# Two transformer blocks on one core: expert 6's down weights in X, an earlier second down product, another order of the last expert loads, fillers in the last step

## The chip, the cores and the metric

One core of a Trainium2 chip. The metric is device time in microseconds of one execution; before the change three runs gave 914.12, 910.62 and 912.9, median 912.9. All times below that are read from a trace are counted from the start of the profiled span.

## The reference, cut to what matters

256 tokens of 1024 channels pass through two blocks. The first block is attention and a Hyena filter, a cross attention, and a mixture of experts; the second an RG-LRU and a block attention, and a mixture of experts. Both mixtures have 32 experts in 4 groups, each token takes two experts of its best group, and each expert is

```python
hdn = silu(x @ w_gate[e]) * (x @ w_up[e])      # 1024 -> 256, twice
y   = (hdn * weight_of_the_token) @ w_down[e]  # 256 -> 1024
```

All in float32. Gate and up weights of one expert are 2048 KB, down weights 1024 KB, so that one expert is 3 MB and the 32 of one mixture 96 MB. All experts are loaded, whatever the router chooses.

## The kernel before, in words

Each mixture runs one expert per step, 32 steps, experts in fixed order in the first mixture and in an order that may turn from step 8 in the second. Five queues (PE, ACT, DVE, POOL, SP) run hand-written programs that meet at semaphores. SP issues the weight transfers.

**Places for weights.** `ring` has four slots of 3 MB (`RING` = 4). The first mixture adds two more places (`apart`: 16 KB rows in `arena` for gate and up, `ROW` and `HT` for down), so it has six (`SIX` = 6), and expert e uses place e % 6. SP's `in_six` (L593) writes the refills: for expert e, wait until gate and up product e - 6 is done (semaphore `gu_done1`), issue gate and up weights, wait until down product e - 6 is done (`down_done1`), issue down weights. The first six experts are asked for ahead of that, the last of them behind the routing product `rt1`. The second mixture has the four slots and, for expert 4, a place made of `HT`, `X` and a part of `arena`. Its first loads are written out up to expert 11 (`first = 3 * RING`); ahead of the loop for experts 12 to 31 stands a `sp.wait_ge(sem("routed"), 3)` (L686).

**PE.** `first_steps` writes out steps 0 to 2, `step_of_six` is a step of the first mixture: turn the gate and up result of the step before (`turn`), turn the gathered rows of the step after (`gather_T`), gate and up product (`gated_up`, 16 matmuls of L1232), scatter the result of e - 2 to the tokens (`onto_tokens`, L1275), gather rows for e + 2 (`gather_rows`, L1198), down product of e - 1 (`brought_down`, L1247). `step` does the like in the second mixture (gate and up L1227, down L1247); it has the rows gathered ahead.

**DVE.** One iteration per step e: `hidden(e - 1)` (it needs gate and up of e - 1 turned by PE), `x_window(e + 1)`, `to_slots(e - 1)`, `low_part(e - 1)`. Four iterations carry a piece more: `extra_counts`, `extra_slots`, `extra_starts`, `extra_experts`, which work out the tiles of experts with more tokens than a window holds. In both mixtures these stand in iterations 4, 5, 6 and 7. In the first mixture they use `X` as scratch, in the second `XN`. `extra_experts` ends with an increment of `routed`. The semaphore gets three increments in the program: `extra_experts` of the first mixture (1), `order_of_steps` of the second in iteration 2 (2), `extra_experts` of the second (3).

```python
                sp.wait_ge(sem("routed"), 3)                        # SP, second mixture, L686
                with sp.Fori(first, NE - RING + 1, RING) as e0:
...
                    if e == RING:                                   # DVE, L2916, both mixtures
                        extra_counts()
...
                    elif e == RING + 3:
                        extra_experts()
```

**Behind the first mixture.** SP loads into freed slots, in this order: `ada10`, `win0`, `ada11`, `win2`, `win3`, ... (2048 KB each). PE runs `ada(10)`, transposes, `ada(11)` (both L903), then the projection with `win0` (L777 to L779). POOL issues the row `final_norm_g` into `ROW` behind a count of down products, and `gates_w` behind the first results of DVE; ACT issues two reads of `bias_rows`.

Of the kernel before, what the change touches and what calls it, by code (L numbers as in the profile page):

```python
# [46 lines left out]
NE = G * EPG  # L47
# [129 lines left out]
GU = 2 * KD * FE  # L177
FEAT = S + 2 * FFN


# [91 lines left out]
def two_blocks(nc, A, out):  # L272

    ctx = ExitStack()
    with ctx:
# [189 lines left out]
        def slot(i):  # L465
            return i % RING

        def arrived(eng, name):
            i = PLACE[name]
            eng.wait_ge(sem(f"slot_full{slot(i)}"), 16 * (i // RING + 1))  # L470
            return ring[:, slot(i), :]

        def vacated(sp, i):

            prev = i - RING
            if prev < 0:
                return
            for b, m in enumerate(MOE_AT):
                if m <= prev < m + RUNG[b]:
                    j = prev - m  # L480
                    sp.wait_ge(sem(f"down_done{b + 1}"), (SIX * (j // RING) + j % RING if b == 0 else j + (j >= RING)) + 1)
# [105 lines left out]
        def _(sp):  # L587
# [4 lines left out]
            def in_six(w):  # L592

                base = MOE_AT[0]

                def refill(e, q, src):
# [7 lines left out]
                    sp.wait_ge(sem("down_done1"), e - (SIX - 1))  # L604
                    if q < RING:
                        sp.dma_start(ring[:, s, GU:SLOT], src[:, GU:SLOT]).then_inc(sem(f"slot_down{q}"), 16)
                    else:
                        sp.dma_start(apart[q - RING][1], src[:, GU:SLOT]).then_inc(sem(f"beside_d{q - RING}"), 16)

                with sp.Fori(SIX, SIX * (NE // SIX) - SIX + 1, SIX) as e0:  # L610
                    for q in range(SIX):
                        refill(e0 + q, q, w[bass.ds(e0 + q, 1)].rearrange("a p f -> p (a f)"))
                for e in range(SIX * (NE // SIX), NE):
                    refill(e, e % SIX, w[e, :, :])

# [5 lines left out]
            def experts(b):  # L621
# [33 lines left out]
                if b == 0:  # L655
                    gate_beside(1, w[RING + 1, :, :])
                    filled("rt1")
                    down_beside(1, w[RING + 1, :, :])
                    in_six(w)
                    return extra_tiles(b, w, slot(base + 2), SIX * (NE // SIX) - RING)  # L660
                filled("rt2")
# [83 lines left out]
        def _(pe):  # L745
# [344 lines left out]
            def moe(b):  # L1090
# [199 lines left out]

                uses_1 = [-(-(NE - q) // SIX) for q in range(SIX)]

                def gate_of_six(n, r):
# [9 lines left out]
                def down_of_six(n, r):  # L1303

                    q, use = r % SIX, r // SIX
                    if q >= RING:
# [15 lines left out]
                def down_arrived(e, r):  # L1322

                    if isinstance(e, int) and e == RING:
                        pe.wait_ge(sem("beside_d0"), 16 * uses_1[RING] + 16)
# [3 lines left out]
                    pe.wait_ge(sem(f"slot_down{q}"), (e - r) * (16 // RING) + more + 16 * uses_1[q])  # L1329
                    return ring[:, slot(base + q), GU:SLOT]  # L1330
# [21 lines left out]
                def first_steps():  # L1352
# [18 lines left out]
                    turn(1)  # L1371
                    gated_up(0, 2)
                    gather_rows(3, 1)
                    onto_tokens(0, 0)
                    gather_T(3)
                    brought_down(0, 1)
                    gather_rows(4, 0)

                def step_of_six(n, r):
# [4 lines left out]
                    if not last:  # L1384
                        gather_T(e + 1)
                    gated_up(n, r)
                    onto_tokens(e - 2, r % 2)
# [788 lines left out]
        def _(dve):  # L2176
# [409 lines left out]
            def moe(b):  # L2586
# [312 lines left out]
                if b == 1:  # L2899
# [7 lines left out]
                    times_up(hb).then_inc(sem("hb1"), 1)  # L2907
                for e in range(3 - b, 2 * RING):
                    if b == 1 and e == 2:
# [4 lines left out]
                    if b == 2 and e == 2:  # L2914
                        order_of_steps()
                    if e == RING:  # L2916
                        extra_counts()
                    elif e == RING + 1:
                        extra_slots()
                    elif e == RING + 2:  # L2920
                        extra_starts()
                    elif e == RING + 3:
                        extra_experts()
# [18 lines left out]

                experts(2 * RING, NE - RING)
                last_step = NE - 1
# [351 lines left out]
        def _(pool):  # L3296
# [58 lines left out]
            pool.wait_ge(sem("mask_row"), 1)  # L3355
            pool.wait_ge(sem("down_done1"), SIX * (NE // SIX) - 1)
            broadcast_row(ROW[:, 0:1024], "final_norm_g", D, "rows")
# [101 lines left out]
```

## Time and profile before

| | us |
|---|---|
| median of three runs | 912.9 |
| profiled execution, its own time | 910.73 |
| its span | 908.9 |
| PE busy in the span | 860.0 (95%) |
| DVE busy | 532.9 (59%) |
| ACT busy | 362.2 (40%) |
| DMA, mean over the span | 314 GB/s |

The span lies 1.8 us under the time of its own execution. PE counts as busy while matmuls are in its pipeline, so its share says little about slack; the DMA row by slices and the waits tell more. The span falls into the first block up to about 300 us, its mixture to about 518, the second block's mixers to about 670, and the second mixture to about 898.

### The profile page before, as it was taken

To read this page: it belongs to the slowest core of one execution; us is meant where nothing else is said; L and a number is where in the kernel's file an instruction comes from. 1 tells how busy PE (TensorE), PEld (TensorE's weight loads), DVE (VectorE), ACT (ScalarE), POOL (GpSimd) and SP (SyncE) were. 2 spreads that over 40 slices of the span, in tenths; PEclk is the share of its full clock that TensorE was granted. 3 is DMA by queue.
4 is the path that set the end of the run, shared out by engine and by line. 5 is a ranking of instruction groups with operands and counts; after the bars stand their busy time and mean duration, and the time that the engine had idled before them with its cause. 6 is when DMAs were issued, how large, how long until landed. Compare 5 with 4: busy or idle time off the path is not lost.

```text
span 908.9 us, 15580 instructions
## 1 busy us (share of the span) xinstructions
PE 860.0 (95%) x5774; PEld 541.0 (60%) x5774; DVE 532.9 (59%) x1182; ACT 362.2 (40%) x711; POOL 22.3 (2%) x41
## 2 busy tenths in 40 slices
PE   8999999999999898999978799999899999999995
PEld 7778558887977333444433389876664555455552
DVE  5877669465455757555554476888754643333335
ACT  5674435455354232333322457745521111111113
POOL 1010111000000000000000000000000000000000
PEclk9999999999999999999999899999999999999998
DMA  9655895546656799999999986630769899999991
GB/s 350 261 192 221 319 393 203 187 176 244 258 204 269 310 368 422 424 426 426 426 424 423 423 317 270 231 140 1 314 228 375 332 412 423 425 425 424 427 416 51
DMA packets 28903, 285.38 MB, mean 314 GB/s; under 512 B 3080, under 2 KB 5544, under 8 KB 7856
## 3 DMA queue, kind: packets, MB, share of 16 engines
q1 hardware_dynamic: 25344, 278.25, 75.6%
q0 software_dynamic: 1136, 3.74, 1.2%
q10 hardware_dynamic: 2368, 2.64, 0.9%
q8 instruction: 36, 0.59, 0.3%
q14 instruction: 19, 0.16, 0.0%
HBM read 283.56 MB, written 1.06 MB: 313 GB/s over the span
## 4 chain that ended last, share of the span: by engine, by line
PE 71%; DVE 12%; DMA 9%; ACT 4%; issue 2%; SPq 0%; DVEq 0%; ACTq 0%
PE bank L1227 13%; PE bank L1247 8%; DMA ring<-in_experts 8%; PE bank L777 8%; PE bank L779 7%; PE bank L778 7%; PE bank L1275 6%; PE bank L1232 4%; DVE ring_r L529 2%; PE bank L1239 2%; PE bank L1198 2%; PE bank L903 1%; PE bank L754 1%; DMA ring<-in_lat 1%; PE bank L868 1%
## 5 line engine op out<-in xcount | busy, mean ns | idle before, releaser
L529 DVE TENSOR_TENSOR ring_r<-ring,ring_r 128x1024 fp32r<-128x1024 f32 (+1 forms) x84 | 99.4, 1212 | 65.4 <-ACT ring_r L522 65.2
L1227 PE MATMUL bank<-ring,arena 128*64 128x256 f32 x992 | 113.9, 382 | 0.6 <-DVE arena L2724 0.6
L522 ACT ACTIVATE ring_r<-ring 128x1024 fp32r<-128x1024 f32 (+1 forms) x84 | 84.9, 1046 | 67.6 <-PE bank L779 66.6
L777 PE MATMUL bank<-HT_r,ring_r 128*128 128x256 f32 x352 | 102.0, 290 | 1.9 <-DVE ring_r L529 1.1
L779 PE MATMUL bank<-HT_r,ring_r 128*128 128x256 f32 x352 | 99.6, 283 | 0.0
L1227 PEld LDWEIGHTS bank<-ring,arena 128*64 128x64 f32 x992 | 68.9, 137 | 36.9 <-issue 5.9
L1247 PE MATMUL bank<-ring,arena 128*64 128x512 f32 (+1 forms) x424 | 83.7, 609 | 1.0 <-issue 0.6
L778 PE MATMUL bank<-XN_r,ring_r 128*128 128x256 f32 x288 | 81.5, 283 | 0.0
L1275 PE MATMUL bank<-arena_r 64*128 64x512 f32 x496 | 75.1, 421 | 2.9 <-DVE arena_r L2808 2.4
L1934 ACT ACTIVATE arena<-bank 128x512 f32<-128x512 f32 (+1 forms) x64 | 31.5, 491 | 113.1 <-PE bank L1227 79.9
L2801 DVE SCALAR_TENSOR_TENSOR arena<-bank,arena 128x512 f32<-128x512 f32 x32 | 24.0, 750 | 83.3 <-PE bank L1247 83.3
L1275 PEld LDWEIGHTS bank<-arena_r 64*128 64x128 f32 x496 | 42.2, 186 | 48.0 <-issue 35.0
L777 PEld LDWEIGHTS bank<-HT_r,ring_r 128*128 128x128 f32 x352 | 67.4, 192 | 5.3 <-issue 5.2
L779 PEld LDWEIGHTS bank<-HT_r,ring_r 128*128 128x128 f32 x352 | 67.5, 192 | 0.0
L1949 ACT ACTIVATE arena_r<-arena 128x512 fp32r<-128x512 f32 x31 | 19.5, 629 | 103.4 <-DVE arena L2801 103.4
L1232 PE MATMUL bank<-ring,arena 128*32 128x512 f32 x352 | 44.0, 619 | 12.5 <-DMA ring<-in_experts 10.2
L2808 DVE SCALAR_TENSOR_TENSOR arena_r<-bank,arena,arena_r 128x512 fp32r<-128x512 f32 x31 | 23.2, 750 | 55.6 <-ACT arena_r L1948 55.6
L778 PEld LDWEIGHTS bank<-XN_r,ring_r 128*128 128x128 f32 x288 | 55.2, 192 | 1.0 <-issue 1.0
L1239 PEld LDWEIGHTS bank<-tab,arena 128*128 128x128 f32 x192 | 19.9, 141 | 52.1 <-issue 51.4
L1247 PEld LDWEIGHTS bank<-ring,arena 128*64 128x64 f32 (+1 forms) x424 | 20.8, 126 | 42.6 <-issue 41.2
L777 PE MATMUL bank<-ring_r,HT_r 128*128 128x512 f32 (+1 forms) x96 | 37.5, 391 | 1.8 <-DVE ring_r L529 1.4
L779 PE MATMUL bank<-ring_r,arena_r 128*128 128x512 f32 x96 | 37.6, 391 | 0.0
(507 smaller groups left out, 1442.0 us busy)
## 6 DMA issues: line engine op xcount, KB each, us to landing
ring<-in_experts SPq DMA_DIRECT2D x53, 2048.0 KB, 13.3
ring<-in_experts SPq DMA_DIRECT2D x53, 1024.0 KB, 10.3
ring<-in_ada SPq DMA_DIRECT2D x12, 2048.0 KB, 10.0
arena<-in_experts SPq DMA_DIRECT2D x10, 2048.0 KB, 16.9
ring<-in_win SPq DMA_DIRECT2D x5, 2048.0 KB, 12.6
ring<-in_hy SPq DMA_DIRECT2D x3, 2048.0 KB, 17.9
HT<-in_experts SPq DMA_DIRECT2D x6, 1024.0 KB, 13.5
ROW<-in_experts SPq DMA_DIRECT2D x5, 1024.0 KB, 13.4
```

Source lines behind the costliest of these rows:

```text
L522: nc.scalar.activation(R(h), w, ACT.Copy).then_inc(sem("w_high"), 1)
L529: nc.vector.tensor_tensor(R(w), w, R(h), ALU.subtract).then_inc(sem("w_low"), 1)
L777: mm(ps, R(ah), R(bh), start=first, stop=False)
L778: mm(ps, R(ah), R(bl), start=False, stop=False)
L779: return mm(ps, R(al), R(bh), start=False, stop=last_)
L1227: last = mm(gu_bank[g * wide:(g + 1) * wide, 0:256], xw[:, k, :], w[k // 4][:, k % 4, g * 256:(g + 1) * 256], start=k == 0, stop=k == KD - 1)
L1232: last = mm(gu_bank[g:g + wide, :], xw[:, 2 * (k % 4) + k // 4, :], w[k // 4][:, k % 4, :], start=k < sides, stop=k >= KD - sides)
L1239: last = tr(guT_bank[:, c * P:(c + 1) * P], gu_sb[:, c * P:(c + 1) * P], ident)
L1247: last = mm(d_bank[g:g + wide, :], hb[:, f, :], w[:, o:o + 512], start=b == 1 or f == 0, stop=b == 1 or f == 1)
L1275: last = mm(acc[2 * t + h][:, :], R(onto[b][rows, i, t * P:(t + 1) * P]), R(u[rows, :]), start=False, stop=False)
L1934: A_(gu_sb[:, 0:gu_cols], gu_bank[:, 0:gu_cols], ACT.Copy).then_inc(sem(f"gu_sb{b}"), 1)
L2801: return V.scalar_tensor_tensor(out=y_gated, in0=(d_bank if bank is None else bank)[:, :], scalar=cur[:, i, 1:2], in1=g2half, op0=ALU.mult ...
```

## The change

- `freed_1` and new place numbers: gate and up of expert e stay at place e % 6. Down weights of expert 6 go to `X`; down weights of the experts behind it go to place (e - 1) % 6, so each waits, in the first round, for one down product fewer.
- SP issues expert 6's down weights to `X` behind the counting product `cns1`, ahead of the refills.
- In the last refills the order is gate and up 30, gate and up 31, down 30, down 31.
- The loads of `ada10`, `win0` and `ada11`, and POOL's `final_norm_g`, wait for one down product more.
- PE: `brought_down(0, 1)` stands straight behind `gated_up(0, 2)`, with a wait for `y_low1`.
- PE: five matmuls of 128x256 (fillers) stand ahead of the gate and up product of the last step.
- DVE: the written-out iterations go to `looped` = (5 - b) * RING, 16 in the first mixture and 12 in the second, and the four extra pieces stand in the last four of them: 12 to 15 in the first, 8 to 11 in the second.

```diff
+        def freed_1(j):
+            q = j % RING
+            e = SIX * (j // RING) + q
+            return max(e, max(d for d in range(SIX + 1, NE) if (d - 1) % SIX == q) if e + SIX >= NE else e + 1)
...
-                with sp.Fori(SIX, SIX * (NE // SIX) - SIX + 1, SIX) as e0:
...
+                refill_gate(SIX, 0, w[SIX, :, :])
+                for e in range(SIX + 1, 2 * SIX + 1):
+                    refill_gate(e, e % SIX, w[e, :, :])
+                    refill_down(e, (e - 1) % SIX, w[e, :, :], SIX + 1)
+                with sp.Fori(2 * SIX + 1, NE - 2 * SIX, SIX) as e0:
...
+                for e in range(NE - SIX - 1, NE - 1):
+                    refill_gate(e, e % SIX, w[e, :, :])
+                    if e == NE - 2:
+                        refill_gate(NE - 1, (NE - 1) % SIX, w[NE - 1, :, :])
+                    refill_down(e, (e - 1) % SIX, w[e, :, :])
+                refill_down(NE - 1, (NE - 2) % SIX, w[NE - 1, :, :])
...
+                    filled("cns1")
+                    sp.dma_start(X[:, :, :].rearrange("p t d -> p (t d)"), w[SIX, :, GU:SLOT]).then_inc(sem("down_in_x"), 16)
                     in_six(w)
...
                     gated_up(0, 2)
+                    pe.wait_ge(sem("y_low1"), 1)
+                    brought_down(0, 1)
                     gather_rows(3, 1)
                     onto_tokens(0, 0)
                     gather_T(3)
-                    brought_down(0, 1)
...
+                    if last:
+                        for _ in range(FILL):
+                            mm(gu_bank[:, 0:256], ident, T("iota")[:, 0:256], start=True, stop=True)
                     gated_up(n, r)
...
-                for e in range(3 - b, 2 * RING):
+                looped = (5 - b) * RING
+                for e in range(3 - b, looped):
...
-                    if e == RING:
+                    if e == looped - 4:
                         extra_counts()
...
-                    elif e == RING + 3:
+                    elif e == looped - 1:
                         extra_experts()
...
-                experts(2 * RING, NE - RING)
+                experts(looped, NE - RING)
...
-            pool.wait_ge(sem("down_done1"), SIX * (NE // SIX) - 1)
+            pool.wait_ge(sem("down_done1"), SIX * (NE // SIX))
```

## Rows read from the trace of the kernel before

**Rows 1.** The page, transfer rate of the core in 40 equal slices.
```profile
GB/s 350 261 192 221 319 393 203 187 176 244 258 204 269 310 368 422 424 426 426 426 424 423 423 317 270 231 140 1 314 228 375 332 412 423 425 425 424 427 416 51
```

**Rows 2.** SP's queue in time: start us, us, issuing line, out<-in.
```profile
307.59 0.34 SPq L601 DMA_DIRECT2D ring<-in_experts  x1
...
313.41 0.33 SPq L601 DMA_DIRECT2D ring<-in_experts  x1
322.80 0.33 SPq L606 DMA_DIRECT2D ring<-in_experts  x1
...
514.25 0.33 SPq L590 DMA_DIRECT2D ring<-in_ada  x1
```

**Rows 3.** Stretches of the first mixture: engines, then PE clock, DMA share, GB/s.
```profile
305.00:310.00 5.00, 4.06 (x32) 1.64 (x32) 3.74 (x19) 2.49 (x5) 0.00 (x0) 1.00 0.31 66
...
320.00:325.00 5.00, 4.50 (x35) 2.04 (x36) 2.60 (x7) 1.74 (x3) 0.00 (x0) 1.00 0.61 205
...
333.00:505.00 172.00, 157.46 (x1272) 63.53 (x1268) 97.68 (x240) 56.97 (x107) 0.58 (x1) 0.99 1.01 424
```

**Rows 4.** PE in time, first mixture and behind; in brackets idle before, releaser.
```profile
317.12 1.92 PE L1232 MATMUL bank<-ring,arena 128*32 128x512 f32 x16 [0.99 <-DVE arena L2601]
...
430.20 1.93 PE L1232 MATMUL bank<-ring,arena 128*32 128x512 f32 x16
...
453.64 1.92 PE L1232 MATMUL bank<-ring,arena 128*32 128x512 f32 x16
...
498.28 1.92 PE L1232 MATMUL bank<-ring,arena 128*32 128x512 f32 x16 [1.48 <-DMA ring<-in_experts]
...
506.96 3.64 PE L1232 MATMUL bank<-ring,arena 128*32 128x512 f32 x16 [4.04 <-DMA ring<-in_experts]
...
514.52 1.06 PE L1247 MATMUL bank<-ring,arena 128*32 128x512 f32 x8 [0.33 <-DVE arena L2746]
...
526.17 1.92 PE L903 MATMUL bank<-ring,cm 128*32 128x512 f32 x16
```

**Rows 5.** PE in time, the matmuls that have the fillers' shape.
```profile
518.15 1.99 PE L754 MATMUL bank<-tab 128*128 128x256 f32 x8
```

**Rows 6.** POOL's and ACT's issues in time, behind the first mixture.
```profile
496.37 0.58 POOL L3323 DMA_DIRECT2D ROW<-in_final_norm_g  x1 [229.78 <-PE bank L1247]
521.49 0.55 POOL L3359 DMA_DIRECT2D ROW<-in_gates_w  x1 [24.54 <-DVE X L3021]
...
523.44 0.41 ACTq L2034 DMA_DIRECT2D arena<-bias_rows  x1
```

**Rows 7.** Transfers issued from 480 to 560 us: count, KB each, median us to landing.
```profile
arena<-bias_rows ACTq DMA_DIRECT2D x1, 1024.0 KB, 14.1
...
ROW<-in_gates_w POOLq DMA_DIRECT2D x1, 512.0 KB, 11.8
```

**Rows 8.** SP's queue in the second mixture, last written-out load and first looped one.
```profile
732.10 0.33 SPq L685 DMA_DIRECT2D ring<-in_experts  x1
733.45 0.33 SPq L693 DMA_DIRECT2D ring<-in_experts  x1
```

**Rows 9.** DVE in time: hidden of step 6, end of extra_experts, hidden of step 10.
```profile
720.09 0.28 DVE L2747 TENSOR_TENSOR arena<-arena,bank 128x128 f32<-128x128 f32 x1
...
721.85 0.13 DVE L2896 CAST tabi<-arena 1x1 int32<-1x1 f32 x1
...
747.96 0.28 DVE L2747 TENSOR_TENSOR arena<-arena,bank 128x128 f32<-128x128 f32 x1
```

**Rows 10.** The chain of waits, gate and up products of experts 12 and 31.
```profile
753.20 3.60 PE bank L1227 x32
...
886.40 3.60 PE bank L1227 x32
```

**Rows 11.** Stretches of the second mixture, columns as in rows 3.
```profile
720.00:885.00 165.00, 165.00 (x1186) 84.21 (x1180) 62.84 (x154) 27.54 (x70) 0.00 (x0) 1.00 1.01 423
...
885.00:886.00 1.00, 1.00 (x10) 0.88 (x9) 0.75 (x1) 0.00 (x0) 0.00 (x0) 1.00 0.75 311
```

More of the change, by code:

```diff
@@ L178 @@
 FEAT = S + 2 * FFN
+FILL = 5
 STAGES = [("f1", 1, (1,)), ("hT", 4, (6, 7, 2, 4)), ("lat", 2, (3, 0)), ("f2", 1, (5,)), ("f3_0", 4, (1, 6, 7, 2)),
@@ L480, in vacated @@
                     j = prev - m
-                    sp.wait_ge(sem(f"down_done{b + 1}"), (SIX * (j // RING) + j % RING if b == 0 else j + (j >= RING)) + 1)
+                    sp.wait_ge(sem(f"down_done{b + 1}"), (freed_1(j) if b == 0 else j + (j >= RING)) + 1)
                     return
@@ L594, in in_six, with refill_gate @@
                 base = MOE_AT[0]
-                def refill(e, q, src):
+                def refill_gate(e, q, src):
                     s = slot(base + q)
@@ L603, in refill, with refill_down @@
                         sp.dma_start(apart[q - RING][0], src[:, 0:GU]).then_inc(sem(f"beside_gu{q - RING}"), 16)
-                    sp.wait_ge(sem("down_done1"), e - (SIX - 1))
+                def refill_down(e, q, src, places=SIX):
+                    sp.wait_ge(sem("down_done1"), e - (places - 1))
                     if q < RING:
-                        sp.dma_start(ring[:, s, GU:SLOT], src[:, GU:SLOT]).then_inc(sem(f"slot_down{q}"), 16)
+                        sp.dma_start(ring[:, slot(base + q), GU:SLOT], src[:, GU:SLOT]).then_inc(sem(f"slot_down{q}"), 16)
                     else:
                         sp.dma_start(apart[q - RING][1], src[:, GU:SLOT]).then_inc(sem(f"beside_d{q - RING}"), 16)
-                with sp.Fori(SIX, SIX * (NE // SIX) - SIX + 1, SIX) as e0:
-                    for q in range(SIX):
-                        refill(e0 + q, q, w[bass.ds(e0 + q, 1)].rearrange("a p f -> p (a f)"))
-                for e in range(SIX * (NE // SIX), NE):
-                    refill(e, e % SIX, w[e, :, :])
+                refill_gate(SIX, 0, w[SIX, :, :])
[3 more added lines that the diff above has]
+                with sp.Fori(2 * SIX + 1, NE - 2 * SIX, SIX) as e0:
+                    for q in range(SIX):
+                        src = w[bass.ds(e0 + q, 1)].rearrange("a p f -> p (a f)")
+                        refill_gate(e0 + q, (q + 1) % SIX, src)
+                        refill_down(e0 + q, q, src)
+                for e in range(NE - SIX - 1, NE - 1):
[4 more added lines that the diff above has]
+                refill_down(NE - 1, (NE - 2) % SIX, w[NE - 1, :, :])
             def half_outside(w, q):
@@ L658, in experts @@
                     down_beside(1, w[RING + 1, :, :])
+                    filled("cns1")
+                    sp.dma_start(X[:, :, :].rearrange("p t d -> p (t d)"), w[SIX, :, GU:SLOT]).then_inc(sem("down_in_x"), 16)
                     in_six(w)
-                    return extra_tiles(b, w, slot(base + 2), SIX * (NE // SIX) - RING)
+                    return extra_tiles(b, w, slot(base + 2), SIX * (NE // SIX) - RING + 1)
                 filled("rt2")
@@ L1291, in moe @@
                 uses_1 = [-(-(NE - q) // SIX) for q in range(SIX)]
+                downs_1 = [-(-(NE - 1 - q) // SIX) for q in range(SIX)]
                 def gate_of_six(n, r):
@@ L1303, in down_of_six @@
                 def down_of_six(n, r):
+                    if r == SIX and isinstance(n, int):
+                        pe.wait_ge(sem("down_in_x"), 16)
+                        return X[:, :, :].rearrange("p t d -> p (t d)")
+                    if r > SIX or not isinstance(n, int):
+                        r = r - 1
                     q, use = r % SIX, r // SIX
@@ L1324, in down_arrived @@
                     if isinstance(e, int) and e == RING:
-                        pe.wait_ge(sem("beside_d0"), 16 * uses_1[RING] + 16)
+                        pe.wait_ge(sem("beside_d0"), 16 * downs_1[RING] + 16)
                         return outside[1]
@@ L1328, in down_arrived @@
                     more = 0 if r < ways and in_turn(e) else 16
-                    pe.wait_ge(sem(f"slot_down{q}"), (e - r) * (16 // RING) + more + 16 * uses_1[q])
+                    pe.wait_ge(sem(f"slot_down{q}"), (e - r) * (16 // RING) + more + 16 * downs_1[q])
                     return ring[:, slot(base + q), GU:SLOT]
@@ L2915, in moe @@
                         order_of_steps()
-                    if e == RING:
+                    if e == looped - 4:
                         extra_counts()
-                    elif e == RING + 1:
+                    elif e == looped - 3:
                         extra_slots()
-                    elif e == RING + 2:
+                    elif e == looped - 2:
                         extra_starts()
-                    elif e == RING + 3:
+                    elif e == looped - 1:
                         extra_experts()
```

## The prediction, made before the changed kernel was run

> **What bounds the kernel now.** I read four views in this order. The page's rate by slices first: the core moves about 424 GB/s from slice 16 to 23, falls to 1 in slice 28, and is at 423 or more again from slice 33 on [rows 1]. These two plateaus are the mixtures; the stages between use less than the bandwidth. Then PE in time, to see which plateau PE waits in. In the first mixture a step costs PE (453.64 - 430.20) / 4 = 5.86 us when it waits for nothing [rows 4], while 3 MB at 424 GB/s take 7.42 us; PE runs ahead on what was loaded early, and in the end waits, 1.48 us at step 30 (498.28) and 4.04 us at step 31 (506.96) [rows 4]. That stage ends on the last weights. In the second mixture gate and up of expert 12 start at 753.20 and of expert 31 at 886.40 [rows 10]: 133.2 us over 19 steps, less 0.84 us for a list product in the last one, is 6.97 us a step, with PE busy all 165 us of the stretch [rows 11]. It is bound by PE, but barely: DMA carries 423 GB/s throughout [rows 11], and 3 MB an expert then take 7.45 us. PE lives on a lead that shrinks by 0.48 us a step. Third, the SP queue, for what starts each transfer. Last, single rows where the change puts a new wait.
>
> **First mixture, the stream of weights.** SP asks for expert 6's gate and up at 307.59, and until then DMA has nothing: 305 to 310 moved 66 GB/s, so (1 - 66/424) x 5 = 4.2 us are lost. A second hole is 320 to 325, 205 GB/s, 2.6 us [rows 3]: the down weights of expert 7 are asked for only at 322.80 and gate and up of 8, queued behind them on SP, later still, though the third gate and up product was over at 319.04 (317.12 + 1.92) [rows 2, 4]. From an issue to full flow I take 1.64 us, an estimate: 205 GB/s in 320 to 325 leave 2.6 us of hole, which fits an end near 321.8 and a new start at 324.44, 1.64 behind 322.80 [rows 2, 3].
>
> Now the changed order. Down 6 (1 MB, 2.47 us) is asked for near 302 and fills part of the first hole. Gate and up 6 flow from 307.59 + 1.64 = 309.23 to 314.17; those of 7, issued 313.41, from 315.05 to 319.99; down 7 no longer waits for the second down product and follows to 322.46. Gate and up 8 can be asked for at about 319.3 and follow without a hole. Before, down 7 flowed from 324.44 to 326.91, so gate and up 8 start 4.45 us earlier. Later places come free in time: gate and up 9 need the fourth gate and up product (near 328.2), and would flow from 329.9, which is when down 8 ends. The cost of the moved down product: the rows for step 3 are gathered 1 us later, which puts step 3 about 0.95 us later. PE's lead over the stream hides it; uncovered it would be 0.95 us. The extra DVE pieces stop PE for some us wherever they stand. In step 12 PE would be at 326.2 + 9 x 5.86 = 378.9, its weights land at 322.46 + 4.94 + 4 x 7.42 = 357.1: a lead of over 20 us hides them, so I count nothing. Stream: 4.4 us earlier; bounds 2.5 (only down 6 counts) and 5.4.
>
> **First mixture, its end.** Gate and up 30 land 4.4 us earlier, and PE starts them at 493.9 instead of 498.28 [rows 4]. Between them and those of 31 stood 1 MB of down 30 (2.47 us) and the row `final_norm_g`, issued 496.37 [rows 6] (0.5 MB, 1.24 us). Both now come behind: gate and up 31 land at 493.85 + 4.94 = 498.8. PE is through step 30 and the turn at about 493.9 + 4.6 = 498.5 (a step's 5.86 less the gathering that the last steps no longer have). Five fillers follow; eight of that shape take 1.99 us, of which the last stays 0.35 us in the pipeline, so 0.23 us each and 1.2 us in all [rows 5]: 0.9 us of them beyond the landing. The product of step 31 starts at 499.7 and takes 1.92 us as at 498.28, not 3.64 as at 506.96, where the wait of 4.04 us had left the granted clock near its 1.2 GHz level [rows 4]. The last down product starts at the later of its hidden values (499.7 + 1.92 + 3.0 = 504.6; before, 3.92 us from 510.60 to 514.52, of which I put 0.9 to the slow clock) and its weights (498.8 + 4.94 + 1.24 = 505.0): 505.0 against 514.52 [rows 4], 9.5 us earlier. Fillers dropped would not change that, as the weights decide.
>
> What is late next: the stream. `ada11` is the third 2 MB behind the experts. Before, issued 514.25 [rows 2], it landed by the order of the stream at 506.9 + 2.47 + 3 x 4.94 = 524.2, and PE used it without a wait at 526.17 [rows 4]. So 2.0 us of slack. With the stream 4.4 us earlier `ada11` lands at 519.8, PE would want it at 526.17 - 9.5 = 516.7 and waits. Besides, `gates_w` (before at 521.49) and the reads of `bias_rows` (523.44), 2 MB together, are issued by engines that run 9.5 us earlier [rows 6], so that they now lie beside `win0` and `ada11`. They took 11.8 and 14.1 us to land [rows 7]; over the 6 to 8 us that overlap I give them about half, 2.3 us of stream time. `ada11` then lands at 522.1, a gain of 4.1 us for all that follows; bounds 1.4 (all 2 MB ahead of it, 4.9 us) and 6.4 (none). The later waits of `ada10` and `win0` are hidden, as both have a queue of over 10 us ahead of them. From here PE has no waits for DMA and the gain is carried to the second mixture.
>
> On that sharing the Trainium skill (DMA: Bandwidth & Descriptors, Queues, rings and completion order) says that each DMA engine goes round-robin between its queue rows, packet by packet. The landing times in rows 7 agree that another queue's transfer neither waits for SP's queue nor overtakes it. By the rule alone, with the small packets of `bias_rows`, those reads would take less than my half, and the gain would be nearer 4.7.
>
> **Second mixture: the step that costs.** SP waits for `routed` = 3 before it asks for the weights of expert 12. Before, `extra_experts` stood in DVE's iteration 7, ended at 721.98 (721.85 + 0.13) [rows 9], and SP came to the wait at 732.4, behind down 11 (732.10), found it fulfilled, and issued at 733.45 [rows 8]. Now it stands in iteration 11, behind `hidden(10)`, whose product was at 747.96; from there to the end of `extra_experts` are 721.98 - 720.09 = 1.89 us [rows 9]. So `routed` = 3 comes at 749.85. SP needs about 1.0 us from the wait to the issue (733.45 - 732.43) [rows 8]: issue at 750.95, flow from 752.6. Before, with the queue never empty, the last 20 experts (60 MB, 62.9 million bytes) ended at 886.3 (the last row shows 0.75 us of activity and the microsecond behind it a third) [rows 11]; at 421 GB/s they take 149.5 us, so gate and up 12 flowed from 736.8. The stream falls back 752.6 - 736.8 = 15.8 us. What absorbs part of it is the lead at the end: gate and up 31 landed 2.47 us before the end, at 883.8, PE wanted them at 886.40 [rows 10], 2.6 us. Price 15.8 - 2.6 = 13.2 us. From the front: expert 12 lands at 757.5 instead of before 753.20, 4.3 us of wait, and then 19 steps of 0.48 us are 9.1, together 13.4. The two agree; I take 13.0, for some tenths in SP's path. All SP loads from 12 on are queued behind the waiting instruction; PE's step 12, and ACT and DVE by it, wait for them. Bounds: 10.5 (the flow resumes 2.5 us sooner) and 16 (the PE lead gone, and a slow clock behind the wait of 4.3 us). That slow clock: after 4.04 us of wait the product took 1.72 us more (3.64 against 1.92) [rows 4]; the same here puts PE behind the stream by a few us, which 0.48 us a step regain by step 31.
>
> Here a rule of the Trainium skill speaks against the change (TensorE: Matmul & The Clock Gate, HAM oscillation): a matmul loop that waits for DMA in every pass can fall to the low clock in every pass. Rows 4 show a product at full speed behind a wait of 1.48 us, so with 0.48 us a step I expect no such thing; were it so, the steps would double to 13.9 us.
>
> **Sum.** Against the profiled execution's own 910.73 us (span 908.9 plus 1.8): -4.1 + 13.0 = +8.9, 919.6. The median of the runs shown is 912.9, 2.2 above that execution; the same difference on it gives 921.8, which I predict.
>
> **Rivals.**
> *The late mark costs nothing (the other side).* Place: L686. The delay is free if expert 12's stream resumes before 736.8 + 2.6 = 739.4, that is if the mark comes by 736.7. Against it: hidden of step 10 cannot exist before 747.96 [rows 9], and nothing in the change touches the wait. For it only that I read the code and have no row of the late mark. Then the first mixture's gain stands alone: 912.9 - 4.1 = 908.8, or 903.4 if its full 9.5 came through. Decides above 739.4. Chance 0.08.
> *The first mixture's full gain comes through.* `ada11` isn't late, the reads don't get in its way: -9.5 + 13.0 = +3.5, 916.4. Against it: 524.2 against 516.7. Chance 0.10.
> *No gain in the first mixture.* `gates_w` and `bias_rows` push `ada11` back, or PE is late in the middle by the extra pieces: +13.0, 925.9. Chance 0.12.
> *Every step of the second mixture at the low clock:* 20 steps x 6 us, about 1,035. Rows 4 speak against it. Chance 0.01.
> Forecast as worked out: 0.69.
>
> **Range.** Terms at their bounds give +4.1 (10.5 - 6.4) to +14.6 (16 - 1.4). From 912.9 that is 917.0 to 927.5; the low end goes down to 914 to take in most of the full-gain case. 914 to 927.5.
>
> **Chances.** A difference under 0.5% (4.6 us) can't be told from none here. Faster by more: most of the case in which the mark costs nothing, 0.06. Within: the rest of it, the full-gain case and a small tail of the forecast, 0.14. Slower: 0.80.
>
> **What would show it.** Right: SP's first L693 issue about 17 us behind L685's sixth instead of 1.35, a hole of about 15 us in the DMA rate near 735 to 750 (4 us earlier by the gain), one PE wait of 3 to 5 us at gate and up 12, then waits of about half a microsecond each step. In the first mixture: no hole at 320, gate and up 31 at full clock, last down product near 505, a PE wait of 3 to 6 us for `ada11`. Wrong: no wait on `routed` in SP's rows, or the second L903 group at 526 as before.

## The result and the profile after

The changed kernel takes 922.08 us (median of four runs, 919.74 to 923.77), the kernel before on the same chip 912.51 (910.62 to 914.12): ratio 1.0104 with a 95% interval of 1.0074 to 1.0134, or 9.5 us slower by the ratio (9.6 by the medians). Forecast were 921.8 and +8.9. The profiled execution of the changed kernel is the slowest of its four: 923.77 us, span 921.9.

About 3 us of its span have nothing to do with the change. Windows of the changed kernel, its start; columns here and below: stretch in us, length, busy us of PE, PEld, DVE, ACT and POOL with instructions, granted PE clock, DMA share, GB/s.

```profile
10.00:20.00 10.00, 10.00 (x41) 8.64 (x40) 7.32 (x16) 6.29 (x12) 0.00 (x0) 0.67 0.99 419
```

Before, the same stretch had a granted clock of 1.00, and the first `ada` load was issued at 25.02; here it is issued at 28.38 (in the twelve other profiles at 25.1 to 25.9). So I count moments from that load in each execution, and give the difference to before:

| | after | after with one number changed (e1_again) |
|---|---|---|
| gate and up 30 start | -3.6 | -5.0 |
| last down product of the first mixture | -8.2 | -9.5 |
| `ada(11)` product | -5.2 | -5.4 |
| first gate and up of the second mixture | -5.0 | -6.2 |
| end of the span | +9.6 | -6.3 |

The first mixture and the stage behind it give about 5 us, the second mixture takes 14.7. The page's rate by slices has the loss in slice 33 of 40, 172 GB/s where it was 412 [rows 1] (the low slices 27 and 28 belong to the second block's mixers and were there before):

```profile
GB/s 352 242 172 205 332 388 213 183 182 240 263 194 284 348 410 421 423 425 424 429 423 422 423 307 210 225 49 91 320 279 405 321 172 429 424 427 423 424 422 57
```

Slice 33 is 738 to 761 us. By windows, after; the first two are the stretches of [rows 3], 305 to 310 and 320 to 325, moved by the 3.36 us of the later start:

```profile
308.36:313.36 5.00, 4.07 (x32) 1.63 (x32) 3.73 (x19) 2.44 (x5) 0.00 (x0) 1.00 0.68 224
323.36:328.36 5.00, 4.13 (x36) 1.74 (x27) 1.74 (x5) 1.13 (x2) 0.00 (x0) 1.00 1.03 439
735.00:740.00 5.00, 5.00 (x38) 2.38 (x36) 2.83 (x8) 0.79 (x2) 0.00 (x0) 1.00 0.31 126
740.00:745.00 5.00, 5.00 (x36) 2.25 (x34) 3.57 (x12) 0.39 (x1) 0.00 (x0) 1.00 0.01 2
745.00:750.00 5.00, 5.00 (x42) 2.84 (x40) 2.46 (x10) 1.18 (x3) 0.00 (x0) 1.00 0.01 2
755.00:760.00 5.00, 2.98 (x14) 1.72 (x16) 0.52 (x2) 0.00 (x0) 0.00 (x0) 0.50 1.03 436
```

The first hole of [rows 3] is filled about half, 224 GB/s for 66, and the second wholly, 439 for 205. A new one of 14.8 us stands between 736.5 (126 GB/s over 735 to 740) and 751.3 (1.64 behind the issue below). Why it is there is shown by DVE's and SP's rows (time, duration, engine, line, operation, tiles). Line numbers have moved: L685 is L707, L693 is L715, L1227 is L1249, L1232 is L1254, L1247 is L1269, L903 is L925.

```profile
746.35 0.28 DVE L2779 TENSOR_TENSOR arena<-arena,bank 128x128 f32<-128x128 f32 x1
748.11 0.14 DVE L2928 CAST tabi<-arena 1x1 int32<-1x1 f32 x1
...
730.43 0.33 SPq L707 DMA_DIRECT2D ring<-in_experts  x1
749.62 0.34 SPq L715 DMA_DIRECT2D ring<-in_experts  x1
```

The mark `routed` = 3 comes with the end of the cast, 748.25, 1.9 us behind the start of the `hidden` of step 10. SP, which was through with its last written-out load at 730.76, issues the first of the loop at 749.62. The waits of SP between 700 and 800 have the line (who waits, for whom: us in total, times, longest; L709 is the loop behind the wait):

```profile
SPq L709 <- DVE tabi L2928: 17.5, 1, 17.5
```

PE pays for it once at expert 12, and from expert 17 (794.10) to expert 30 in every step ("[... <-DMA" is the wait ahead of the group):

```profile
757.01 5.44 PE L1249 MATMUL bank<-ring,arena 128*64 128x256 f32 x32 [5.50 <-DMA ring<-in_experts]
765.76 3.67 PE L1249 MATMUL bank<-ring,arena 128*64 128x256 f32 x32
...
786.67 3.67 PE L1249 MATMUL bank<-ring,arena 128*64 128x256 f32 x32
794.10 3.67 PE L1249 MATMUL bank<-ring,arena 128*64 128x256 f32 x32 [0.39 <-DMA ring<-in_experts]
...
875.46 3.67 PE L1249 MATMUL bank<-ring,arena 128*64 128x256 f32 x32 [0.36 <-DMA ring<-in_experts]
884.10 3.67 PE L1249 MATMUL bank<-ring,arena 128*64 128x256 f32 x32 [1.61 <-DMA ring<-in_experts]
891.51 3.67 PE L1249 MATMUL bank<-ring,arena 128*64 128x256 f32 x32 [0.37 <-DMA ring<-in_experts]
899.34 3.67 PE L1249 MATMUL bank<-ring,arena 128*64 128x256 f32 x32
```

From 765.76 to 786.67 PE still goes at its own 6.97 us a step. From 794.10 to 875.46 are 11 steps of 7.40 us: 3 MB at 425 GB/s. The stage was bound by PE at 6.97 us a step [rows 10, 11]; from expert 17 on it is bound by DMA.

The end of the first mixture answers to [rows 4]:

```profile
498.02 1.92 PE L1254 MATMUL bank<-ring,arena 128*32 128x512 f32 x16 [1.47 <-DMA ring<-in_experts]
502.49 2.32 PE L1417 MATMUL bank<-tab 128*128 128x256 f32 x10
504.74 1.92 PE L1254 MATMUL bank<-ring,arena 128*32 128x512 f32 x16
509.71 1.06 PE L1269 MATMUL bank<-ring,arena 128*32 128x512 f32 x8 [0.34 <-DVE arena L2778]
517.70 3.12 PE L925 MATMUL bank<-ring,cm 128*32 128x512 f32 x16 [2.36 <-DVE st L3063]
524.34 1.92 PE L925 MATMUL bank<-ring,cm 128*32 128x512 f32 x16 [1.19 <-DMA ring<-in_ada]
```

With 3.36 us taken off for the later start, the last down product is at 506.35 instead of 514.52 and `ada(11)` at 520.98 instead of 526.17: of 8.2 us there are 5.2 left.

### The profile page after: what moved, and what is told of

Its sections match the earlier page's. It is cut to its first block, busy times and chain, and to the rows that moved or that the text cites. A ratio compares the mean times of both kernels' runs of the same rounds, so it can differ in the third digit from the quotient of the medians.

```text
span 921.9 us, 15486 instructions
## 1 busy us (share of the span) xinstructions
PE 865.0 (94%) x5784; PEld 550.3 (60%) x5784; DVE 532.3 (58%) x1182; ACT 362.0 (39%) x711; POOL 22.2 (2%) x41
## 4 chain that ended last, share of the span: by engine, by line
PE 63%; DMA 16%; DVE 12%; ACT 4%; issue 3%; SPq 1%; DVEq 1%; ACTq 0%
DMA ring<-in_experts 14%; PE bank L799 8%; PE bank L1249 7%; PE bank L801 7%; PE bank L800 7%; PE bank L1269 6%; PE bank L1254 4%; PE bank L1297 4%; PE bank L1220 2%; DVE ring_r L536 2%; PE bank L1261 2%; DMA ring<-in_ada 1%; PE bank L925 1%; PE bank L1226 1%; PE bank L890 1%
## 5 line engine op out<-in xcount | busy, mean ns | idle before, releaser
L1249 PE MATMUL bank<-ring,arena 128*64 128x256 f32 x992 | 115.7, 386 | 12.4 <-DMA ring<-in_experts 11.8
L1249 PEld LDWEIGHTS bank<-ring,arena 128*64 128x64 f32 x992 | 74.9, 138 | 45.5 <-issue 12.9
L1269 PE MATMUL bank<-ring,arena 128*64 128x512 f32 (+1 forms) x416 | 81.7, 600 | 1.0 <-issue 0.6
L1254 PE MATMUL bank<-ring,arena 128*32 128x512 f32 x352 | 42.3, 598 | 4.6 <-DMA ring<-in_experts 2.3
L1269 PEld LDWEIGHTS bank<-ring,arena 128*64 128x64 f32 (+1 forms) x416 | 20.4, 125 | 42.6 <-issue 40.3
```

Of the source, the lines that this page charges most:

```text
L1249: last = mm(gu_bank[g * wide:(g + 1) * wide, 0:256], xw[:, k, :], w[k // 4][:, k % 4, g * 256:(g + 1) * 256], start=k == 0, stop=k == KD - 1)
L1254: last = mm(gu_bank[g:g + wide, :], xw[:, 2 * (k % 4) + k // 4, :], w[k // 4][:, k % 4, :], start=k < sides, stop=k >= KD - sides)
L1269: last = mm(d_bank[g:g + wide, :], hb[:, f, :], w[:, o:o + 512], start=b == 1 or f == 0, stop=b == 1 or f == 1)
```

## The experiments

Each time is a median beside the kernel before on the same chip, with the ratio and its 95% interval. "Base" is e1: the changed kernel with the one number of e1. The disputed price first.

**e1, e1_again: the loop does not wait for the late mark.** The entries of the table that SP reads are written before the second increment.

```diff
-                sp.wait_ge(sem("routed"), 3)
+                sp.wait_ge(sem("routed"), 2)
```

> The changed kernel with one number changed: SP waits for routed = 2 ahead of its loop over experts 12 to 31, not for 3. DVE's extra pieces stay in iterations 8 to 11. Theory (SP's late mark is the whole price of the second mixture, 14.6 us in the trace): 922.1 - 14.6 = 907.5 us, no hole in DMA near 740, gate and up 12 start 27.9 us behind those of expert 8 (4 steps of 6.97), no wait there. Rival (the pieces themselves, now in iterations 8 to 11, hold up DVE and through it PE): the time stays above 915 with waits of PE on DVE in steps 8 to 12. Rival (the late start of the stream has another cause on SP): the hole stays.

Measured: 905.87 (904.91 to 909.09) against 911.43, ratio 0.9939 (0.9925 to 0.9953); on another chip, with twelve runs,

> The changed kernel with the wait for routed = 2 once more, as the base on the same chip as the two kernels with it: 0.994 of the kernel before, 905 to 907 us.

906.92 against 910.85, 0.9959 (0.9944 to 0.9973). In e1's windows the hole is gone:

```profile
740.00:745.00 5.00, 5.00 (x34) 2.27 (x32) 3.05 (x10) 0.90 (x2) 0.00 (x0) 1.00 1.01 424
```

One number turns +1.0% into -0.4 to -0.6%. So the wait of SP is what makes the changed kernel slower; the difference of the ratios, 0.0145 to 0.0165, is 13 to 15 us.

**e2: the pieces of the second mixture back in iterations 4 to 7, the wait kept.**

```diff
-                looped = (5 - b) * RING
+                looped = (6 - 2 * b) * RING
```

> The changed kernel with the extra pieces of the second mixture back in iterations 4 to 7 (looped = 16 in the first mixture, 8 in the second), the wait for routed = 3 kept. Theory: the mark comes near 720 and SP finds it there; 907.5 us, the same as with the wait for 2 within 1 us. If the pieces cost something of their own in 8 to 11, this one is faster than the wait for 2 by that much. Against the kernel before it shows the first mixture's changes alone: 4 to 6 us faster.

Measured: 907.67, 0.9960 (0.9944 to 0.9975). The mark early removes the loss as not waiting for it does. The medians of e1 and e2 on this chip are 1.8 us apart, more than the 1 us expected, but the intervals overlap and e1_again has nearly the ratio of e2; pieces that cost something of their own in iterations 8 to 11 would have made e2 the faster one.

**e3: the kernel before with nothing but the late pieces in the second mixture.**

```diff
+                looped = (1 + b) * RING
-                    if e == RING:
+                    if e == looped - 4:
                         extra_counts()
```

> The kernel before with only this change: the pieces of the second mixture in iterations 8 to 11 (the first mixture keeps 4 to 7). Theory: the late mark alone, 912.5 + 14.6 = 927.1 us, SP's first looped load about 17 us later, a PE wait of 4 to 6 us at gate and up 12. Rival (the two parts interact, the price exists only with the first mixture's changes): under 920.

Measured: 924.21 (923.5 to 926.9), 1.0148 (1.0127 to 1.0168). The first mixture is that of before, and the price appears all the same: 12.8 us by the medians, 13.5 by the ratio, and 14.1 in the trace from the first gate and up of the second mixture to the end, for the 14.6 expected. Up to there this kernel does what the one before does, and yet its profile is 0.9 us ahead: so much do two profiles differ by themselves. Its SP and PE:

```profile
SPq L687 <- DVE tabi L2896: 17.4, 1, 17.4
...
757.99 5.21 PE L1227 MATMUL bank<-ring,arena 128*64 128x256 f32 x32 [5.15 <-DMA ring<-in_experts]
```

**e10: how the price grows.** The changed kernel with the pieces of the second mixture one iteration earlier, in 7 to 10.

```diff
-                    if e == looped - 4:
+                    if e == looped - 4 - (b - 1):
```

> The changed kernel with the extra pieces of the second mixture one iteration earlier, 7 to 10 instead of 8 to 11; the wait for routed = 3 stays. The mark comes one step, 6.97 us, earlier. Theory (price = how late the stream resumes less the lead PE has at the end): 6.97 us less, 922.1 - 7.0 = 915.1 us, SP's first looped load 6.97 us earlier, the wait at gate and up 12 gone (5.5 - 7.0 below zero) and PE waits only from about step 15 on. Rival (the price is the one long wait and the slow clock behind it, about 7 us): nearly all of 14.6 us gone, about 908.

Measured: 914.04 against 911.37, 1.0029 (1.0018 to 1.0041). Its SP and its first wait:

```profile
727.54 0.33 SPq L707 DMA_DIRECT2D ring<-in_experts  x1
739.69 0.34 SPq L715 DMA_DIRECT2D ring<-in_experts  x1
...
776.83 3.67 PE L1249 MATMUL bank<-ring,arena 128*64 128x256 f32 x32 [0.25 <-DMA ring<-in_experts]
```

PE has no wait at step 12 here, and is overtaken at step 16. Counted from the first gate and up of the second mixture in each execution, SP's first load of the loop comes at 61.15 us before, 71.95 in e10, 79.0 in the changed kernel, and the stage from there to the end of the span takes 236.6, 244.1 and 251.3. A lateness of 10.8 us costs 7.5, one of 17.85 costs 14.7: 3.3 and 3.2 us are free, the rest is paid one for one. Without the late mark the same stretch takes 236.5 to 237.6 us in the ten profiles of the other runs on base, so that each of these figures is good to about a microsecond.

**e4: no fillers.** Base, `FILL = 5` to `FILL = 0`.

> The changed kernel with SP's wait for routed = 2 (905.9 us, called the base here) and no fillers ahead of the last gate and up product. Theory (weights decide the end of the mixture, and ada11 behind it): the product of step 31 starts about 1.2 to 2.2 us sooner, the wait ahead of it is under a microsecond so that it keeps the full clock, the last down product by its weights or hidden values at most 2 us sooner, and nothing of it arrives behind ada11: within 0.7 us of the base. Rival (the fillers keep the clock): a 3.6 us product, 1.5 us or more slower.

Measured: 906.36 against 911.14, 0.9942 (0.9924 to 0.9959).

```profile
500.02 1.92 PE L1254 MATMUL bank<-ring,arena 128*32 128x512 f32 x16 [1.24 <-DMA ring<-in_experts]
505.98 1.06 PE L1269 MATMUL bank<-ring,arena 128*32 128x512 f32 x8 [1.33 <-DMA ring<-in_experts]
```

Without them PE waits 1.24 us and the product of step 31 still takes 1.92 us. It starts 5.87 us behind the product of step 30 (494.15), with the fillers 6.72 us behind it (493.74 to 500.46 in e1_again): they take PE's wait and run 0.85 us beyond it. That is hidden, as without them the last down product waits 1.33 us for its weights, and starts 11.83 us behind the product of step 30, with them 11.68. They neither cost nor give anything that can be measured.

**e5: gate and up 31 behind down 30 again.** Base, with the two requests in the old order.

```diff
-                    if e == NE - 2:
-                        refill_gate(NE - 1, (NE - 1) % SIX, w[NE - 1, :, :])
                     refill_down(e, (e - 1) % SIX, w[e, :, :])
+                refill_gate(NE - 1, (NE - 1) % SIX, w[NE - 1, :, :])
                 refill_down(NE - 1, (NE - 2) % SIX, w[NE - 1, :, :])
```

> The base with the last loads in the old order: gate and up 30, down 30, gate and up 31, down 31. Theory: gate and up 31 land 2.5 us later, the last down product 2 to 4 us later, but ada11 lands when it did, as the bytes ahead of it are the same: total within 1 us of the base. Rival (the end of the mixture carries through): 2.5 us or more slower.

Measured: 906.73, 0.9952 (0.9933 to 0.9970). In its profile the first refill was 1.7 us later than in e4 beside it, and gate and up 30 by 1.8. The last down product comes 6.1 us earlier than before, 9.0 in e4; 1.8 of the difference go with the refill, which leaves 1.1 for the order, less than the 2 to 4 us expected and hardly more than two profiles differ by. At the second mixture's first gate and up e5 has 4.6 us, e4 3.9, in spite of the refill. So the order moves the last down product by a microsecond or less, and nothing of it is seen behind `ada11`.

**e6: the second down product back in its old place.** Base, `brought_down(0, 1)` behind `gather_T(3)`.

> The base with the second down product back behind the scatter. Theory: down 8 waits about 2.5 us longer on SP but the queue holds gate and up 8 then, so the hole does not come back (down 7 no longer waits for that product): stream and total within 0.7 us of the base, step 3 about 1 us earlier. Rival (it is this move that closes the hole at 320): 2.5 us slower.

Measured: 904.96 (904.72 to 906.02), 0.9925 (0.9902 to 0.9948), the lowest time of all. With both changes of place for weights in, the moved product brings nothing: gate and up 9 are asked for 19.8 us behind gate and up 6 in e6 (327.55 - 307.76) and 20.9 in e1_again (328.75 - 307.90, and the like in the other profiles with the moved product), since PE's work of step 3 comes about a microsecond later with it. The intervals of e6 and of base overlap, so that it is faster than base isn't shown; that the edit is not needed is.

**e7: expert 6's down weights not ahead of gate and up 6, but behind.** Base otherwise.

```diff
+                sp.dma_start(X[:, :, :].rearrange("p t d -> p (t d)"), w[SIX, :, GU:SLOT]).then_inc(sem("down_in_x"), 16)
```

> The base with expert 6's down weights asked for behind its gate and up weights, not ahead: the first hole of DMA isn't used. Theory (the stream's start decides when ada11 lands): 2.47 us lost less the 0.9 us gap behind gate and up 6, so gate and up 30 and ada11 1.6 to 2.5 us later, total 1.6 to 2.5 us above the base. Rival (the gain comes from the end of the mixture): no difference.

Measured: 908.62, 0.9958 (0.9942 to 0.9975): by the ratio not to be told from base, by the medians 1.7 us above e1_again. The 1.6 to 2.5 us expected are neither shown nor excluded. Windows of e7:

```profile
305.00:310.00 5.00, 3.63 (x31) 1.41 (x31) 3.77 (x18) 2.68 (x4) 0.00 (x0) 1.00 0.25 54
330.00:335.00 5.00, 5.00 (x44) 1.81 (x44) 1.77 (x5) 1.54 (x3) 0.00 (x0) 1.00 1.05 436
```

and of base (e1_again):

```profile
305.00:310.00 5.00, 4.00 (x32) 1.63 (x32) 3.83 (x18) 2.68 (x4) 0.00 (x0) 1.00 0.69 223
330.00:335.00 5.00, 5.00 (x44) 2.02 (x38) 2.16 (x4) 1.93 (x4) 0.00 (x0) 1.00 0.96 360
```

Base moves (223 - 54) x 5 = 845 KB more in the first stretch, worth 2.0 us, and loses part of it in the other, (436 - 360) x 5 = 380 KB or 0.9 us, where the queue waits for the gate and up product held back by the moved down product. At gate and up 30 the two differ by 1.1 us.

**Where the 9 us at the end of the first mixture shrink to 5.** e8 keeps PE busy with 12 fillers ahead of `ada(11)`, for its clock; e11 does so with 6; e9 puts `ada(11)` behind the projection with `win0`. All on base.

> The changed kernel with the wait for routed = 2, and 12 matmuls of 128x256 ahead of ada(11), where PE waits for that load. They take 2.8 us, less than the wait of about 4 us. Theory (the wait for ada11 costs twice: the wait, and a product and some matmuls at the low clock behind it): L925 at 1.92 us instead of up to 3.64, 1.5 to 2.3 us faster than the base where its wait was long, on average 1 to 2. Rival: no difference.

> The changed kernel with the wait for routed = 2 and 6 instead of 12 matmuls of 128x256 ahead of ada(11). A trace showed that each takes two records of 0.23 us, so 12 took 5.35 us and ran past the landing by 2.5 us; 6 take 2.7 us and end before it. Theory: L925 at 1.92 us in every execution, up to 2 us faster than the same kernel without them (906.5), 905.5 in the median. Rival (the execution time hangs on other clock events as much): within 0.7 us of 906.5.

> The changed kernel with the wait for routed = 2, and ada(11) and its column product moved behind the projection with win0 (ACT's copy of its result moved likewise). If ada11's landing is what holds back the gain of the first mixture, PE starts the projection as soon as win0 is split, near 521, and the total falls by 2 to 4 us below the base, to about 903. If something else holds it (win0, the split on ACT and DVE, final_norm_g), less than 1 us.

Measured: e8 908.89, 0.9970 (0.9956 to 0.9984); e11 905.88, 0.9942 (0.9927 to 0.9957); e9 906.47, 0.9946 (0.9929 to 0.9963). In e8 I had the fillers wrong in size:

```profile
518.44 5.35 PE L776 MATMUL bank<-tab 128*128 128x256 f32 x24
```

A matmul of this float32 shape is two records of 0.22 us, so 12 took 5.35 us where I had reckoned 2.8 from [rows 5]; they reached past the landing of the weights, and e8 tests nothing but that. In e11 the six fit:

```profile
519.60 2.76 PE L776 MATMUL bank<-tab 128*128 128x256 f32 x12
522.28 1.92 PE L925 MATMUL bank<-ring,cm 128*32 128x512 f32 x16
```

What they guard against is seen in e2 and, without it, in e1_again:

```profile
521.64 3.64 PE L925 MATMUL bank<-ring,cm 128*32 128x512 f32 x16 [4.05 <-DMA ring<-in_ada]
```
```profile
513.08 3.58 PE L925 MATMUL bank<-ring,cm 128*32 128x512 f32 x16 [2.04 <-DVE st L3063]
521.23 1.92 PE L925 MATMUL bank<-ring,cm 128*32 128x512 f32 x16 [2.67 <-DMA ring<-in_ada]
```

Over the profiles of the changed kernel and its variants, `ada(11)` took 3.64, 3.41, 3.44 and 2.75 us behind waits of 4.05 (e2), 3.71 (e4), 3.19 (e7) and 2.83 (e1), and 1.92 behind waits of 2.67, 2.49 (e6), 2.33 (e10), 2.24 (e5) and 1.19 (after). The wait is mostly shorter where `ada(10)` before it ran at the low clock, as in e1_again's first row (1.19, 2.49 and 2.67 us behind a slow one, 2.33 to 4.05 behind one of 1.92): that seems to cost nothing, as PE would wait for `ada11` anyway. Where `ada(11)` is the slow one, a gain of 4.6 us there has shrunk to 3.2 at the second mixture's first load in e2, while in e1_again 5.4 grew to 6.2; e4 (slow, 4.6 to 3.9) and e11 (fast, 4.8 to 5.6) go the same two ways. Base does now the one, now the other, which may be part of its scatter (904.51 to 910.95); that it is was not shown, for e11's interval overlaps base's two, and its median lies within 0.7 us of the 906.5 that its expectation compares with. In e9 PE goes from the transposes straight to the projection and waits for DVE there:

```profile
521.13 0.36 PE L799 MATMUL bank<-HT_r,ring_r 128*128 128x256 f32 x1 [1.91 <-DVE XN_r L3099]
```

The wait for `ada11` is replaced by one for DVE's split of the values, and `ada(11)` now costs its 1.92 us in a stretch where PE has work. The 2 to 4 us that e9 would have given if `ada11` alone held the stage did not come. e9 and e11 differ by 0.6 us in median, with overlapping intervals.

## Why the prediction was right

The forecast of 921.8 met 922.08, and its two terms were each close. That they met to 0.3 us is luck: in the traces the first part gave 5.0 us for 4.1 and the second cost 14.7 for 13.0, two errors of opposite sign, and the four runs lie 4 us apart. Point by point:

*The stream of the first mixture, 4.4 us earlier: right within the scatter.* In seven executions with all the edits that bear on the stream and no late first refill (after, e1_again, e2, e4, e8, e9, e11), gate and up 30 start 3.6, 5.0, 4.9, 4.6, 4.8, 4.3 and 4.5 us earlier. The first hole is filled in part and the second wholly, as reckoned. That the moved down product costs nothing was wrong: e6 has 5.8 us without it. I had it hidden by PE's lead, but SP's queue waits for the same gate and up products. My own reckoning had the place, the request for gate and up 9 just as the queue runs dry (329.9); that left no room for 1 us of delay, and the dip at 330 to 335 in base is what it cost.

*The last down product, 9.5 us earlier: right* (8.2 in the changed kernel, 8.8 to 9.5 in e1_again, e2, e4, e8, e9 and e11). What comes last there was a close call, as in the sum (504.6 against 505.0): the hidden values in the changed kernel (0.34 us behind DVE), the weights without fillers (e4).

*Fillers, 1.2 us: wrong, 2.32.* [Rows 5] count x8 records, and I took a record for a matmul. They run 0.85 us past PE's wait, for the 0.9 reckoned, but only because that wait is 1.24 us without them and not 0.3; the last down product does not see it, so that the error cost nothing. e4 shows also that they were not needed: a product behind a wait of 1.24 us takes 1.92 us, like that behind 1.48 us in [rows 4].

*`ada11` gives 4.1 of the 9.5 us on: right as a place, low in size.* `ada(11)` comes 5.2 us earlier in the changed kernel and 4.6 to 5.4 in e1_again, e2, e4 and e11. The whole gain by the ratios of e1, e1_again, e2 and e4 is 5.6, 3.7, 3.6 and 5.3 us, around and above the 4.1. The Trainium skill (DMA: Bandwidth & Descriptors, Queues, rings and completion order) says that each DMA engine takes its queue rows in turn, packet by packet. From that I had worked out that the reads of `bias_rows` take less of the stream than half their size, and a gain of 4.7; the traces, 4.6 to 5.4, lie on both sides of that, and don't decide it. I did not see two things. `final_norm_g` is now asked for at 502.67, and DVE waits for it ahead of the first values of the next stage, 1.37 us in e2, hidden, it seems, behind `ada11`. It is 1.82 us in the changed kernel. And the wait for `ada11` can leave PE at the low clock, which costs what e2 lost, about 1.5 us. The rival in which the full 9.5 us come through fell, as did the one without any gain.

*The second mixture, +13.0: right in mechanism, 1.7 us low in the changed kernel (14.7) and 1.1 in e3 (14.1).* The lateness of SP's request was right: 17.5 forecast, 17.85 measured, of which SP's path from mark to issue is 1.37 us (749.62 - 748.25) for 1.0; the sum's 750.95 is also 0.1 above its own 749.85 + 1.0. What failed is the step on what absorbs part of it: my sum left 17.5 - 13.0 = 4.5 us free, and 3.2 are. It had two parts, both off (and 0.2 on top for SP's path). The first was the slack of the queue before the change, 736.8 - 733.45 - 1.64 = 1.7 us, by a rate of 421 GB/s. The changed kernel's stream starts on an empty queue and so gives the rate: from 749.62 + 1.64 = 751.26 to 899.27 (last row below) are 148.0 us for 62.9 million bytes, 425 GB/s. By that rate the flow of expert 12 began at 738.3 before, and the slack was 3.2 us. The second was the lead at the end, 2.6 us, from the end of the flow to PE's start. But PE starts on the landing. Gate and up 30 of the changed kernel had flowed at 899.27 - 9.88 (down 30, gate and up 31 and down 31, 4 MB at 425 GB/s) = 889.4, and PE, waiting for them, began at 891.51: 2.1 us behind. Of the 2.6 some 0.5 are left. Both together, 3.2 + 0.5, stand against 3.2 measured, which is within what two profiles differ by. The 1.5 us gained by the one error made good most of the 2.1 lost by the other. That the lead at the end is so small is seen without the late mark too: in e7 PE waits 0.64 and 0.37 us at experts 29 and 30, in e6 0.44 and in e1 0.37 us at expert 30.

```profile
899.00:900.00 1.00, 1.00 (x10) 0.75 (x11) 0.31 (x1) 0.80 (x2) 0.00 (x0) 1.00 0.28 115
```

*The wait at step 12 and those behind it: right, a little short in size.* Forecast 3 to 5 us, then half a microsecond a step; measured 5.50, then none for four steps, then 0.28 to 0.44 us, once 1.61 (expert 29), the products behind them all at the full clock. The product behind the 5.50 us took 5.44 us instead of 3.67, at a granted clock of 0.50 over 755 to 760. As reckoned, the stream was then ahead of PE, for four steps, and PE caught up with it. The Trainium skill (TensorE: Matmul & The Clock Gate, HAM oscillation) tells of a matmul loop that waits for DMA in every pass and starts every pass at the low clock. Here 14 products behind waits of 0.28 to 1.61 us all took 3.67 us, so with waits this short it did not happen.

*The rival on the other side, the late mark costs nothing, fell* with e1, e2 and e3, which take it away, take it away in another manner, and add it alone. Its threshold was too high by a microsecond: it had 739.4 - 1.64 - 733.45 = 4.3 us of lateness free, and 3.2 to 3.3 are.

What stays open: the share of the X load (about a microsecond of stream by e7, under what the times can tell), and whether e6 and e11 together would be faster than either. No run takes back the new places of the down weights alone, to which the reckoning gives the second hole, nor the later waits of `ada10`, `win0`, `ada11` and `final_norm_g`, nor the pieces of the first mixture in iterations 12 to 15: that the gain of the first mixture comes from the places is argued from the holes. The changed kernel's profile also loses 1.1 us against before between the second mixture's first load (-6.1) and its first gate and up (-5.0), where e1_again loses none; no run was made for that, and it is near what two profiles differ by.

## What to carry to other kernels

When a piece of work is moved to a later place for the sake of one stage, look who waits for its last increment in every other stage that runs the same code: here the edit fitted the first mixture, where nobody but a far-off reader waits, and stopped SP's queue for 17 us in the second, where a wait had stood for a mark that it didn't need (asking for the second increment gives 905.9 us on one chip and 906.9 on another, 0.6 and 0.4% under the kernel before, instead of 1% over it).

A stage that is bound by PE with DMA at full rate has almost no slack for DMA. Its step of 6.97 us stood against 7.40 us of weights, and about 3 us of lateness used up what there was; every microsecond beyond was paid in full.

When several edits serve the same stage, take each away by itself: of the four taken away here (the down weights in X, the moved down product, the order of the last loads, the fillers) none is seen in the total, and the moved product cost about a microsecond on another queue.

## What the runs showed of the hardware

- PE goes on some time behind the end of a flow, and a lead read from the rate of the stream is too long by that. Reckoned from 751.26 at 425 GB/s, it was 0.8 us for gate and up 12 of the changed kernel (756.2 to 757.01), 0.9 for 28 (874.6 to 875.46), and 2.1 for 29 and 30 (889.4 to 891.51 for 30). The jump is the wait of 1.61 us at 884.10, where the twelve before have 0.28 to 0.44; e3 has one of 1.04 at 892.37, e10 one of 1.39 at 874.11. Why the last ones come so late is open.
- `ada(11)` took 1.92 us behind waits up to 2.67 us in these profiles, and 2.75 to 3.64 behind waits of 2.83 to 4.05. That is no rule for the length of the wait: `ada(10)`, of the same form, took 1.92 us behind 2.59 in e9 and 3.31 behind the same 2.59 in e11, and 3.58 behind only 2.04 in e1_again (granted clock 1.00 over 512 to 513, 0.53 over 513 to 516). Of the two, a slow first one mostly went with a fast second one, and the profiles with a slow second one lost 0.7 to 1.5 us from there to the second mixture's first load (e1, e2, e4, e7), where those with a fast one won 0.9 (after, e1_again, e5, e6, e8, e10, e11).
- The first gate and up product of the first mixture can be slow behind one and the same wait. In e1 and in e1_again, the same kernel:

```profile
305.89 3.35 PE L1254 MATMUL bank<-ring,arena 128*32 128x512 f32 x16 [1.29 <-issue]
...
305.92 1.93 PE L1254 MATMUL bank<-ring,arena 128*32 128x512 f32 x16 [1.29 <-issue]
```

  SP's refills wait for that product, and the first came 1.4 us later in e1. One profile of each kernel is not enough to read differences of a microsecond or two.
